# The heads phase of an mLSTM layer: memory products two slots sooner, chunk statistics behind each slot's urgent work, a third row buffer, and the last chunk's tiles in spent value room

## The chip, the cores and the metric

One core of a Trainium2 chip runs the whole program in one launch. The metric is device time in microseconds; before the change three runs gave a median of 3094.31 us (3094.05 to 3098.62). TensorE is PE in the profile (PEld its weight loads), VectorE DVE, ScalarE ACT, GpSimd POOL, and SyncE SP, which here only issues DMAs.

## The reference

Two layers on 1024 prompt tokens and 32 sample tokens (8 batches of 4). Each layer is a token mixer, a layer norm, a squared-ReLU MLP and a layer norm; layer 0 mixes by a Conformer convolution, layer 1 by mLSTM with 4 heads of width 512. The change lies in the mLSTM heads:

```python
num = a * (q @ C) + s @ v            # s = (q k^T) * exp(d - m), causal
den = a * (q @ n) + sum(s)
h = num / max(|den|, exp(-m))
C_new = decay * C + (k * w)^T @ v    # prompt and 8 sample states, [512, 512] each
# per head, over its 512 columns:
hn = (h - mean(h)) * rsqrt(var(h) + eps) * norm_g
out = sigmoid(o_pre) * (hn + skip * xc)      # then out @ w_down
```

## The kernel before

The four heads run one after the other. A head first makes queries, keys and values and the prompt's own memory (some 50 us), then goes through 16 **slots**, in which three kinds of work are laced together. The order on every engine is written out by hand in `phase_b_pe`, `phase_b_act`, `phase_b_dve` and `phase_b_pool`: each engine takes its list in order, and semaphores tie the lists.

- **Attention steps.** 14 steps (`SLOTS`; slots 2 and 3 have none and add the carried memory instead, `carried`, 8 matmuls twice a slot). For step r PE makes `scores` (L1567), DVE weights them (`weighted`, L2053, tile PT), ACT rounds them (`high`, L1819, PH), DVE takes the rest (`low`, L2075, PL) and PE adds `values` (L1582 to L1584, 12 matmuls). Scores run two steps ahead of values. ACT's `weights` (L1828, exponentials) run three ahead.
- **Memory products.** 16 halves of the 8 sample states (`HALVES`), by `memory` and `new_memory`: the first half of a batch starts with `old_memory` (L1614, PE reads the state tile CT), and each half has two products (L1639), which DVE folds into CT (`update`, L2045). States come and go by DMA through three CT buffers, 1 MB each way.
- **Chunk statistics.** The prompt's rows come in four chunks of 256 tokens (tc 0, 1, 2 and END), the sample rows are DEC. When a chunk's last step is done (`LAST`: slots 1, 5, 9, 15), a chain runs over the engines: `denominators` (PE L1603), `den_part` (ACT L1705), `bound` (DVE L2177); `raw_out` (ACT L1723 or L1720) takes the numerators out of PSUM; `sum_tiles` 1 (DVE), `head_mean` (PE L1448), `center` (DVE L2206), `square` (ACT L1731), `sum_tiles` 2 (DVE, ends in L2199), `head_var` (PE L1453), `root` (ACT L1737, a table load and a square root into SD), `inverse` (DVE L2211), `normalise` (DVE L2217), `gain` (ACT L1746), `skip` (DVE L2232), `gate` (DVE L2240), and `out_store` by POOL (L1403). The denominator of one chunk shares its PSUM bank with the variance of the chunk before, so `denominators` waits for that chunk's `root` (semaphore hsd). The statistics of DEC and END are finished inside the next head, between its query and token products (L1479, L1502).

Before, the chunks alternate between two row buffers HT0 and HT1, and `raw_out` waits until the row stored two chunks earlier has left (o_out). After the last head comes the down projection (`down`, `product` at L447 to L449; `beside` puts the last statistics among its matmuls). POOL splits its weight panels (`split_panel`, L432 and L434) into space that the heads used, so each panel also waits for whatever lay there.

## Time and profile before

| | us |
|---|---|
| median of three runs | 3094.31 |
| the profiled execution | 3095.94 |
| its span in the profile | 3094.2 |
| PE busy | 2968.4 (96%) |
| DVE busy | 1687.0 (55%) |
| ACT busy | 846.0 (27%) |
| POOL busy | 1069.2 (35%) |

The profile is one execution. A busy share is a mean over stages: the heads phase runs from about 1590 to 2142 us of the span, the down projection and the second MLP follow. A row of the timeline gives start and duration in us, engine, line, what is written and read, and in square brackets how long the engine had been idle and what ended it.

### The profile page before, as it was taken

Reading aid. Unit: us, or ns where it says so; the run is one execution under the profiler, and the core shown is the slowest. Engines: PE = TensorE matmul, PEld = TensorE weight load, DVE = VectorE, ACT = ScalarE, POOL = GpSimd, SP = SyncE. Lnnn points to the kernel's source line nnn. Section 1 sums busy time; section 2 is a strip of 40 time slices with the busy share of each in tenths; the row PEclk is TensorE's granted clock in tenths of the full one; section 3 lists DMA queues with packets and bytes.
Section 4 is the critical chain, followed back from the end, with each engine's and each line's share of the span. In section 5 each row is a group of like instructions: output and inputs, shape, how many; then the busy total and the mean of one; then the engine's idle time right before and its main releaser. Section 6 shows DMA issues by size and latency. Waiting matters only on the chain.

```text
span 3094.2 us, 50087 instructions
## 1 busy us (share of the span) xinstructions
PE 2968.4 (96%) x19348; PEld 2748.6 (89%) x19348; DVE 1687.0 (55%) x2551; ACT 846.0 (27%) x1491; POOL 1069.2 (35%) x742
## 2 busy tenths in 40 slices
PE   7998899999999999999989989897999999999997
PEld 7885789999999998999967768675998999999997
DVE  5877445544444455344357887877226444444445
ACT  4000542222212224111144434434006122222211
POOL 3232023555565523333200111102332365555553
PEclk9999899999999999999989999998999999999999
DMA  8555211111111113433244563839310111111121
GB/s 229 138 142 141 80 50 42 40 42 50 51 54 47 55 35 108 141 105 104 90 171 178 188 229 137 298 119 328 118 42 28 55 55 41 37 44 48 53 75 57
DMA packets 276673, 313.20 MB, mean 101 GB/s; under 512 B 25733, under 2 KB 217477, under 8 KB 275314
## 3 DMA queue, kind: packets, MB, share of 16 engines
q1 hardware_dynamic: 257777, 250.82, 26.7%
q10 hardware_dynamic: 13048, 40.28, 3.4%
q0 software_dynamic: 5712, 20.19, 1.8%
q8 instruction: 97, 1.59, 0.2%
q14 instruction: 39, 0.32, 0.0%
HBM read 219.91 MB, written 92.19 MB: 101 GB/s over the span
## 4 chain that ended last, share of the span: by engine, by line
PE 82%; DVE 8%; ACT 3%; issue 3%; DMA 2%; PEld 1%; POOL 0%; SPq 0%; another core or an unknown queue 0%; ACTq 0%; DVEq 0%; POOLq 0%; PEldq 0%
PE ps L447 19%; PE ps L448 19%; PE ps L449 19%; PE ps L882 3%; PE ps L881 3%; PE ps L883 3%; PE ps L1502 2%; PE ps L1567 2%; PE ps L2564 2%; PE ps L1523 1%; PE ps L1593 1%; PE ps L1525 1%; PE ps L1524 1%; DVE CT L2045 1%; PE ps L1639 1%
## 5 line engine op out<-in xcount | busy, mean ns | idle before, releaser
L447 PE MATMUL ps<-AH,WH 128*128 128x352 f32 x3072 | 999.1, 325 | 4.9 <-POOL WL L434 2.0
L449 PE MATMUL ps<-AH,WL 128*128 128x352 f32 x3072 | 985.3, 321 | 0.0
L448 PE MATMUL ps<-AL,WH 128*128 128x352 f32 x3072 | 985.2, 321 | 0.0
L447 PEld LDWEIGHTS ps<-AH,WH 128*128 128x128 f32 x3072 | 576.7, 188 | 30.3 <-issue 23.9
L448 PEld LDWEIGHTS ps<-AL,WH 128*128 128x128 f32 x3072 | 577.9, 188 | 1.1 <-issue 0.2
L449 PEld LDWEIGHTS ps<-AH,WL 128*128 128x128 f32 x3072 | 576.9, 188 | 0.0
L432 POOL TENSOR_SCALAR WH<-RAW 128x1024 fp32r<-128x1024 f32 x152 | 181.0, 1191 | 950.5 <-PEq L454 751.4
L434 POOL TENSOR_TENSOR WL<-RAW,WH 128x1024 fp32r<-128x1024 f32 x152 | 401.1, 2639 | 12.7
L1105 DVE TENSOR_TENSOR X<-X,ps 128x352 f32<-128x352 f32 x432 | 225.1, 521 | 264.6 <-PE ps L883 134.1
L996 ACT ACTIVATE SGF<-ps 128x352 f32<-128x352 f32 x192 | 88.9, 463 | 679.7 <-PE ps L449 679.6
L1057 DVE TENSOR_TENSOR HR<-SGF 128x352 f32<-128x352 f32 x144 | 92.7, 644 | 288.5 <-ACT SGF L996 286.6
L447 PE MATMUL ps<-HH,WH 128*128 128x352 f32 x768 | 249.6, 325 | 0.0
L449 PE MATMUL ps<-HH,WL 128*128 128x352 f32 x768 | 246.3, 321 | 0.0
L448 PE MATMUL ps<-HL,WH 128*128 128x352 f32 x768 | 246.0, 320 | 0.0
L742 POOL TENSOR_TENSOR WL<-RAW,WH 128x1024 fp32r<-128x1024 f32 x48 | 117.2, 2441 | 182.1 <-ACT WH L768 181.1
L2994 DVE SCALAR_TENSOR_TENSOR CB<-U,PR,CB 128x32 f32<-128x32 f32 (+3 forms) x180 | 155.4, 922 | 0.7
L447 PEld LDWEIGHTS ps<-HH,WH 128*128 128x128 f32 x768 | 144.1, 188 | 2.7 <-issue 2.3
L448 PEld LDWEIGHTS ps<-HL,WH 128*128 128x128 f32 x768 | 144.3, 188 | 0.4
L449 PEld LDWEIGHTS ps<-HH,WL 128*128 128x128 f32 x768 | 144.0, 187 | 0.0
L758 POOL TENSOR_TENSOR WL<-RAW,WH 128x1024 fp32r<-128x1024 f32 x48 | 116.9, 2435 | 45.0 <-ACT WH L771 44.0
L881 PE MATMUL ps<-HH,WH 128*128 128x352 f32 x384 | 123.6, 322 | 0.0
L882 PE MATMUL ps<-HL,WH 128*128 128x352 f32 x384 | 123.6, 322 | 0.0
(376 smaller groups left out, 4921.6 us busy)
## 6 DMA issues: line engine op xcount, KB each, us to landing
RAW<-in_ffn_w SPq DMA_DIRECT2D x128, 512.0 KB, 3.8
CT<-in_state_mlstm_C SPq DMA_DIRECT2D x32, 1024.0 KB, 6.8
out_C_s<-CT SPq DMA_DIRECT2D x32, 1024.0 KB, 7.7
RAW<-in_ml_w_in SPq DMA_DIRECT2D x32, 512.0 KB, 3.9
RAW<-in_conv_w_pw SPq DMA_DIRECT2D x24, 512.0 KB, 8.3
STK<-u_scratch SPq DMA_DIRECT2D x64, 184.0 KB, 3.8
xc_scratch<-XC ACTq DMA_DIRECT2D x16, 528.0 KB, 2.7
so_scratch<-SO ACTq DMA_DIRECT2D x16, 528.0 KB, 3.7
```

The lines of the kernel that those rows point to most:

```text
L432: pool.tensor_scalar(WH[:, k % 4], RAW[:, k % 2], 1.0, 0.0, ALU.mult, ALU.add).then_inc(w_hi, 1)
L434: pool.tensor_tensor(WL[:, k % 4], RAW[:, k % 2], WH[:, k % 4].bitcast(F32), ALU.subtract).then_inc(w_split, 1)
L447: pe.matmul(ps[:, bank, 0:CW], wh[:, k, cols], hi[:, k, cs], start=(k == 0), stop=False)
L448: pe.matmul(ps[:, bank, 0:CW], wh[:, k, cols], lo[:, k, cs], start=False, stop=False)
L449: mm = pe.matmul(ps[:, bank, 0:CW], wl[:, k, cols], hi[:, k, cs], start=False, stop=(k == nk - 1))
L742: pool.tensor_tensor(WL[:, 2 * g % 4], raw, WH[:, 2 * g % 4].bitcast(F32), ALU.subtract).then_inc(w_split, 1)
L758: pool.tensor_tensor(WL[:, (2 * g + 1) % 4], raw, WH[:, (2 * g + 1) % 4].bitcast(F32), ALU.subtract).then_inc(w_split, 1)
L881: pe.matmul(ps[:, bank, 0:CW], wh, hi(k), start=(start and k == 0), stop=False, skip_group_check=True)
L882: pe.matmul(ps[:, bank, 0:CW], wh, lo(k), start=False, stop=False, skip_group_check=True)
L883: mm = pe.matmul(ps[:, bank, 0:CW], wl, hi(k), start=False, stop=(k == 1), skip_group_check=True)
L1105: dve.tensor_tensor(x, x, ps[:, bank, 0:CW], ALU.add).then_inc(F.acc, 1)
L2994: ins = dve.scalar_tensor_tensor(y, x(t), w, y, ALU.mult, ALU.add)
```

## The change

The memory halves move two slots ahead and are spread: one half each in slots 0 and 1, two each in slots 2 and 3, one each in 4 to 13. Each chunk's denominators move one slot later, to the head of the slot, and the chain behind them one slot later too (on DVE behind the slot's updates and weighted scores, where before most of it stood ahead of them). The next head's block weights move from slot 12 to slot 0. The rows of chunk 2 lie in the first half of XO0 in place of HT0, so the gates' load for END waits for the store of chunk 2. In the last head, END's rows (HTL) and its loads (XOL) lie where the values were, and `raw_out` of END waits for no store; POOL splits the first two panels before it stores chunk 2 and splits the next two before it stores DEC and END. `head_mean` of DEC goes from ahead of the down projection to the middle of its first product.

```diff
-        HALVES = {2: (0, 1), 3: (2, 3), 4: (4, 5)} | {q: (q + 1,) for q in range(5, 15)}
-        IS_STEP = 13
+        HALVES = {0: (0,), 1: (1,), 2: (2, 3), 3: (4, 5)} | {q: (q + 2,) for q in range(4, 14)}
+        IS_STEP = 12
@@ ht, xo_load
+            if tc == END and h == HEADS - 1:
+                return HTL[:]
+            return (HT0, HT1, XO0[:, 0], None, HT0)[tc][:, :, 0:TC[tc][1]]
+            if tc == END and h < HEADS - 1:
+                pool.wait_ge(o_out[0], 16 * (3 * h + 2))
+            elif tc == END:
+                pool.wait_ge(pv_mm, NS * HEADS)
@@ phase_b_pe
                 for n, tc in enumerate((0, 1, 2, END)):
-                    if q == LAST[tc] and n != 1:
+                    if q == LAST[tc] + (tc != END):
                         denominators(n, FINAL[tc])
...
-                if q == LAST[1]:
-                    denominators(1, FINAL[1])
...
-                    if q == LAST[tc] + 3:
+                    if q == LAST[tc] + 4:
                         head_var(pe, h, tc)
@@ raw_out
-            if row_half(h, tc) and tc != DEC:
-                wait(act, o_out[1], 16 * (2 * h + (tc == END)))
-            else:
-                wait(act, o_out[0], 16 * (3 * h + (0, 0, 1, 0, 2)[tc]))
+            if tc < 2:
+                wait(act, o_out[1], 16 * 2 * h)
+            elif tc == 2:
+                wait(act, hskip, 5 * h)
+            elif tc == DEC:
+                wait(act, o_out[0], 16 * 3 * h)
+            elif h < HEADS - 1:
+                act.wait_ge(o_out[0], 16 * (3 * h + 1))
@@ phase_b_act
-                    if n == 2:
+                    if n == 3:
                         square(act, h, tc)
-                    if n == 3:
+                    if n == 4:
                         root(act, h, tc)
-                    if q == LAST[tc] + 4:
+                    if q == LAST[tc] + 5:
                         gain(act, h, tc)
@@ phase_b_dve: taken from the slot's head
-                    if n == 2:
-                        center(dve, h, tc)
-                    if n == 3:
-                        sum_tiles(dve, h, tc, 2)
-                    if n == 4:
-                        inverse(dve, h, tc)
-                    if n == 6:
-                        gate(dve, h, tc)
@@ behind the first update and weighted
-                    if q == LAST[tc] + 1:
+                    if n == 1:
                         sum_tiles(dve, h, tc, 1)
+                    if n == 5:
+                        inverse(dve, h, tc)
@@ at the slot's end
+                    if n == 2:
+                        center(dve, h, tc)
+                    if n == 3:
+                        sum_tiles(dve, h, tc, 2)
-                    if n == 4:
+                    if n == 5:
                         normalise(dve, h, tc)
-                    if n == 5:
+                    if n == 6 and not (tc == 2 and h == HEADS - 1):
                         skip(dve, h, tc)
+                    if n == 7:
+                        gate(dve, h, tc)
-                if q == 12:
+                if q == 0 and h < HEADS - 1:
@@ behind the last slot
+            if h == HEADS - 1:
+                skip(dve, h, 2)
+            gate(dve, h, 2)
```

Three places show how it moves instructions; head 1 is the one shown. First, PE around the denominators of chunk 1. The names are PS for the summed weights, SQH for the squares' sums, XCH and QT for keys and queries, CT for a state. Before:

```order
5248 L1614 MATMUL ps<-CT,QZ 32x512 [waits ct_in0]
5249 L1614 MATMUL ps<-CT,QZ 32x512 x3
5250 L1639 MATMUL ps<-VM,WKS 128x512 [waits upd_ev,vm_done]
5251 L1567 MATMUL ps<-QT,XCH_133 128x256 [waits p_done]
5252 L1567 MATMUL ps<-QT,XCH_133 128x256 x3
5253 L1603 MATMUL ps<-PS,ones_63 128x256 [waits hsd,hcent,psum_done]
5254 L1639 MATMUL ps<-VM,WKS 128x512 [waits upd_ev]
```

And in the change (the first 12 matmuls behind the variance are step 3's values):

```order
5255 L1648 MATMUL ps<-VM,WKS 128x512 [waits upd_ev]
5256 L1462 MATMUL ps<-SQH,ones_h 128x256 [waits hsum]
5257 L1591 MATMUL ps<-PH,VH 128x128 [waits p_lo]
...
5269 L1612 MATMUL ps<-PS,ones_63 128x256 [waits hsd,hcent,psum_done]
5270 L1623 MATMUL ps<-CT,QZ 32x512 [waits ct_in1]
5271 L1623 MATMUL ps<-CT,QZ 32x512 x3
5272 L1648 MATMUL ps<-VM,WKS 128x512 [waits upd_ev,vm_done]
5273 L1576 MATMUL ps<-QT,XCH_133 128x256 [waits p_done]
```

The denominators stood behind a state's products and a step's scores; now they stand ahead of both, 12 narrow matmuls behind the variance whose root they wait for.

Second, DVE at the end of the head, from the last weighted scores to the sums of DEC (SQD, DND) and END (SQH). Before:

```order
973 L2075 TENSOR_TENSOR PL<-PT,PH 128x128 [waits pv_mm,p_hi]
974 L2217 TENSOR_TENSOR HT_157<-HT_157,RST 128x1024 [waits hrst]
975 L2045 SCALAR_TENSOR_TENSOR CT<-CT,ROWB,ps 128x512 [waits upd_mm] x2
976 L2232 SCALAR_TENSOR_TENSOR HT_157<-XCH_133,PRM,HT_157 128x256 [waits hgain]
977 L2232 SCALAR_TENSOR_TENSOR HT_157<-XCH_133,PRM,HT_157 128x256 x3
978 L2240 TENSOR_TENSOR HT_157<-HT_157,XO_154 128x1024 [waits xo_in0,hskip]
979 L2177 TENSOR_TENSOR DND<-DND,ROWB 128x32 [waits den_abs]
980 L2192 TENSOR_TENSOR SQD<-HTD 128x64 [waits num_ev,hvar]
```

In the change:

```order
977 L2086 TENSOR_TENSOR PL<-PT,PH 128x128 [waits pv_mm,p_hi]
978 L2223 RECIPROCAL RST<-SD 128x256 [waits hsd]
979 L2229 TENSOR_TENSOR XO_157<-XO_157,RST 128x1024 [waits hrst]
980 L2244 SCALAR_TENSOR_TENSOR XO_157<-XCH_133,PRM,XO_157 128x256 [waits hgain]
981 L2244 SCALAR_TENSOR_TENSOR XO_157<-XCH_133,PRM,XO_157 128x256 x3
982 L2189 TENSOR_TENSOR DND<-DND,ROWB 128x32 [waits den_abs]
983 L2204 TENSOR_TENSOR SQD<-HTD 128x64 [waits num_ev,hvar]
...
986 L2252 TENSOR_TENSOR XO_157<-XO_157 128x1024 [waits xo_in0,hskip]
```

The reciprocal stood ahead of the last step's scores; now it stands behind them, no update separates the chain's links any more, and DEC's sums follow the skip.

Third, POOL behind the last head. HT_157 in row 269 is chunk 2. Before:

```order
269 L1403 DMA out_scratch<-HT_157 128x4x256 [waits hout]
270 L1395 DMA XO_154<-xc_scratch 128x4x256 [waits hout]
271 L1396 DMA XO_154<-so_scratch 128x4x256
272 L432 TENSOR_SCALAR WH<-RAW 128x1024 [waits w_free,w_raw0,upd_mm,p_lo]
...
277 L1403 DMA out_scratch<-HT_157 128x4x256 [waits hout]
278 L432 TENSOR_SCALAR WH<-RAW 128x1024 [waits w_free,w_raw0,hvar,o_out0]
```

In the change, where XO_157 in row 273 is chunk 2:

```order
269 L434 TENSOR_SCALAR WH<-RAW 128x1024 [waits w_free,w_raw0,upd_mm,p_lo]
...
271 L434 TENSOR_SCALAR WH<-RAW 128x1024 [waits w_free,w_raw1,o_out1,dexp]
...
273 L1415 DMA out_scratch<-XO_157 128x4x256 [waits hout]
274 L1407 DMA XOL<-xc_scratch 128x4x256 [waits pv_mm,hout]
275 L1408 DMA XOL<-so_scratch 128x4x256
276 L434 TENSOR_SCALAR WH<-RAW 128x1024 [waits w_raw0,w_free,o_out0]
```

Two panels are split before chunk 2 is stored, and the third panel no longer stands behind the store of END.

## Rows read from the trace of the kernel before

**Rows 1.** The page: span and PE's share.
```profile
span 3094.2 us, 50087 instructions
PE 2968.4 (96%) x19348; PEld 2748.6 (89%) x19348; DVE 1687.0 (55%) x2551; ACT 846.0 (27%) x1491; POOL 1069.2 (35%) x742
```
**Rows 2.** Windows: stretch, its length, busy us (instructions) by engine, clock, DMA, GB/s.
```profile
1780.80:1862.20 81.40, 73.13 (x428) 55.38 (x428) 67.54 (x122) 32.13 (x68) 8.04 (x11) 0.98 0.71 246
1866.00:1916.00 50.00, 49.32 (x287) 41.19 (x285) 38.83 (x80) 24.02 (x52) 4.81 (x7) 1.00 0.42 145
2141.70:2154.90 13.20, 0.82 (x4) 0.60 (x4) 8.88 (x8) 1.08 (x4) 10.51 (x7) 0.60 1.03 411
```
**Rows 3.** PE's waits in head 1's slots, 1780 to 1863: total, times, longest.
```profile
PE ps L1453 <- DVE SQH L2199: 3.1, 2, 1.6
...
PE ps L1603 <- ACT SD L1737: 1.8, 1, 1.8
```
**Rows 4.** Timeline of the weight loads of PE, head 1, slots 4 to 10.
```profile
1800.05 0.16 PEld L1614 LDWEIGHTS ps<-CT,QZ 128*32 128x32 f32 x8 [0.35 <-issue]
...
1825.08 0.30 PEld L1453 LDWEIGHTS ps<-SQH,ones_h 128*128 128x128 f32 x2 [2.05 <-DVE SQH L2199]
1828.96 0.30 PEld L1603 LDWEIGHTS ps<-PS,ones 128*128 128x128 f32 x2 [1.96 <-issue]
...
1830.87 3.17 PEld L1567 LDWEIGHTS ps<-QT,XCH 128*128 128x128 f32 x8
...
1835.85 1.73 PEld L1567 LDWEIGHTS ps<-QT,XCH 128*128 128x128 f32 x8
```
**Rows 5.** Timeline of DVE, head 1, slot 8.
```profile
1824.60 0.43 DVE L2199 SCALAR_TENSOR_TENSOR SQH<-DN,SQH 128x256 f32<-128x256 f32 x1
1824.94 0.74 DVE L2045 SCALAR_TENSOR_TENSOR CT<-CT,ROWB,ps 128x512 f32<-128x512 f32 x1
1825.60 0.42 DVE L2053 TENSOR_TENSOR PT<-ps,DT 128x256 f32<-128x256 f32 x1
```
**Rows 6.** Timeline of ACT, head 1, slot 8.
```profile
1826.05 0.41 ACT L1819 CAST PH<-PT 128x256 fp32r<-128x256 f32 x1 [3.04 <-DVE PT L2053]
1826.36 0.69 ACT L1828 ACTIVATE DT<-ROWB,BT 128x128 f32<-128x128 f32 x2
1827.08 1.28 ACT L1737 ACT_TABLE_LOAD   x1
1828.37 0.47 ACT L1737 ACTIVATE SD<-ps,tiny 128x256 f32<-128x256 f32 x1
```
**Rows 7.** Groups by line in head 1's slots: busy us, mean ns, idle before.
```profile
L2211 DVE RECIPROCAL RST<-SD 128x256 f32<-128x256 f32 x3 | 5.2, 1749 | 1.7 <-ACT SD L1737 1.7
...
L1746 ACT ACTIVATE HT<-HT,PRM 128x256 f32<-128x256 f32 x12 | 5.1, 499 | 1.4 <-DVE HT L2217 1.4
L2232 DVE SCALAR_TENSOR_TENSOR HT<-XCH,PRM,HT 128x256 f32<-128x256 f32 x12 | 5.0, 477 | 0.5 <-ACT HT L1746 0.5
```
**Rows 8.** Timeline of PE's weight loads where head 2 begins.
```profile
1863.94 0.32 PEld L1448 LDWEIGHTS ps<-SQD,ones_h 128*128 128x128 f32 x2 [0.28 <-issue]
...
1868.57 0.30 PEld L1453 LDWEIGHTS ps<-SQD,ones_h 128*128 128x128 f32 x2 [0.70 <-DVE SQD L2199]
```
**Rows 9.** PE's waits from 2140 to 2300 us.
```profile
PE ps L447 <- ACT HT L1720: 7.5, 1, 7.5
PE ps L1448 <- DVE SQD L2194: 4.9, 1, 4.9
```
**Rows 10.** Timeline from 2143 us: the last END rows, the third panel's first product.
```profile
2154.17 1.08 ACT L1720 COPY HT<-ps 128x512 f32<-128x512 f32 x2 [12.12 <-DMA out_scratch<-HT]
...
2184.21 0.40 PE L447 MATMUL ps<-AL,WH 128*128 128x352 f32 x1 [3.61 <-POOL WL L434]
```
**Rows 11.** The chain that ended last, head 3: start, us, what.
```profile
2084.10 8.96 DMA out_C_s<-CT
2093.08 15.23 DMA CT<-in_state_mlstm_C
```

More of the change, by code:

```diff
@@ L1284, in halves_at @@
             return [(n // 2, n % 2) for n in HALVES.get(q, ())]
-        def row_half(h, tc):
-            return 1 if tc == 1 or tc == END and h < HEADS - 1 else 0
         def store_sem(h, tc):
@@ L1369, in ht @@
         def ht(h, tc):
-            return HTD[:] if tc == DEC else HT[row_half(h, tc)][:, :, 0:TC[tc][1]]
+            if tc == DEC:
+                return HTD[:]
+            if tc == END and h == HEADS - 1:
+                return HTL[:]
+            return (HT0, HT1, XO0[:, 0], None, HT0)[tc][:, :, 0:TC[tc][1]]
         def squares(tc):
@@ L1377, in summed, with xo @@
             return 10 * h + (2 * tc + n if tc < 3 else 5 + 2 * n + (tc == END))
-        def xo(tc, m):
-            return (XOD0, XOD1)[m][:] if tc == DEC else XO[tc % 2][:, m if tc != 1 else 0, :, 0:TC[tc][1]]
+        def xo(h, tc, m):
+            if tc == DEC:
+                return (XOD0, XOD1)[m][:]
+            if h == HEADS - 1 and tc == END:
+                return XOL[:, m]
+            if h == HEADS - 1 and tc == 2 and m == 0:
+                return XCL[:]
+            return XO1[:, 0] if tc == 1 else XO0[:, m]
         def reloaded(h, tc):
@@ L1422, in phase_b_pool @@
             vm(2)
-            vm(3)
-            vm(4)
-            vm(5)
+            for b in range(3, 7):
+                vm(b)
             out_store(pool, h, 0)
             xo_load(pool, h, 2)
-            vm(6)
             vm(7)
             out_store(pool, h, 1)
-            xo_load(pool, h, 3)
-            out_store(pool, h, 2)
-            xo_load(pool, h, 4)
+            xo_load(pool, h, DEC)
             if h < HEADS - 1:
+                out_store(pool, h, 2)
+                xo_load(pool, h, END)
                 out_store(pool, h, DEC)
@@ L1442, in head_mean @@
             pe.wait_ge(num_ev, 5 * h + tc + 1)
-            if tc in (DEC, END):
-                pe.wait_ge(den_abs, 5 * h + tc + 1)
+            pe.wait_ge(den_abs, 5 * h + tc + 1)
             if tc != DEC:
@@ L2492, in _ @@
             split_panel(pool, NP_D + 1, NR_D // 2 + 1, 1, NQ_D + 1)
+            out_store(pool, HEADS - 1, 2)
+            xo_load(pool, HEADS - 1, END)
+            pool.wait_ge(o_out[0], 16 * 11)
+            split_panel(pool, NP_D + 2, (NR_D + 2) // 2 + 1, 2, NQ_D + 2)
+            pool.wait_ge(hvar, 20)
+            split_panel(pool, NP_D + 3, (NR_D + 3) // 2 + 1, 3, NQ_D + 3)
             out_store(pool, HEADS - 1, DEC)
             out_store(pool, HEADS - 1, END)
-            pool.wait_ge(o_out[0], 16 * 12)
-            pool.wait_ge(hvar, 20)
-            for k in range(2, 4):
-                split_panel(pool, NP_D + k, (NR_D + k) // 2 + 1, k, NQ_D + k)
             with pool.Fori(1, 4) as i:
@@ L2691, in beside @@
                 if (c, h, k) == (0, 0, KT // 2):
+                    head_mean(pe, HEADS - 1, DEC)
                     pe.wait_ge(wd_lo, 2)
@@ L2713, in down @@
                         between(c, n - 6)
-            head_mean(pe, HEADS - 1, DEC)
             pe.wait_ge(upd_ev, 4 * DEC_B * HEADS)
```

22 lines of the change are left out of this document (11 added, 11 removed).

## Prediction

> **What bounds the kernel now.** I read the page first: PE is busy for 96% of a span of 3094.2 us [rows 1], so almost everywhere the time is PE's own work, and a change of order can only give or take the places where PE waits. Then the windows over one head. In head 1's slots PE is busy 73.1 of 81.4 us and DVE 67.5; right behind them, where the next head makes its queries and tokens, PE is busy 49.3 of 50 us [rows 2]. So the slots hold some 8 us of PE idle per head, and whatever delays PE at a head's edge is paid in full, as there is no idle behind it to absorb it. Then the waits. In the slots PE waits 3.1 us in two variances for DVE's sums and 1.8 us in one set of denominators for ACT's square root [rows 3]; the timeline puts these at 1825.08 and 1828.96 [rows 4]. The last place is behind head 3: from 2141.7 to 2154.9 PE is busy 0.8 of 13.2 us, at a mean clock of 0.60 [rows 2]. There it waits 4.9 us for the sums of DEC, then 7.5 us for ACT's copy of END's numerators, and later 3.6 us for the third weight panel [rows 9, 10]. The copy itself had waited 12.1 us for a DMA, the store of chunk 2's rows out of the buffer it writes [rows 10].
>
> **The tail of the heads phase.** With its own buffer the END copy no longer waits for a store. What is late next: ACT's order is gain of chunk 2, DEC's numerators and denominators, the second rounding of the down projection's input, END's denominators, END's copy. In the new order (worked out below) chunk 2's gain ends 0.9 us behind PE's last value product, the other four take about 2.9 us, and PE starts the down projection 3.5 to 4 us behind its last value product: at about 2145.8 in before's clock, counted without the three heads ahead, against 2154.9. `head_mean` of END in that product will wait 2 us, since DVE now does skip and gate of chunk 2 ahead of END's sums. The third panel waits for chunk 2's store and no longer for END's; issued near 2149.5 it should have landed and been split by 2165, before the six first products end at about 2171.6, so the 3.6 us go too. Before, the seventh product starts at 2184.2 [rows 10]. That is -12.6 us; a clock drop of 3.4 us just behind it, worth 1.7, may go with the wait. I take **-14 us** for the tail, last head's own slots included; its bounds are 0 (the copy is held by something else, such as the rounding) and -16.0, the sum of the three waits [rows 9, 10].
>
> **The slots.** I walked head 1 through the new lists by hand, each instruction starting when its engine is free and its inputs are there, with durations and latencies from the trace: an update 0.66 (from 1824.94 to 1825.60), weighted scores 0.4 behind their matmuls, a step's scores 1.73, and so on [rows 4 to 7]. The starting point is the end of the first two scores, 1780.8, which the change leaves alone.
>
> *Gains.* Slots 0 and 1 take one memory half each, whose four updates (2.6 us) fall where DVE waited for PE. Slot 4 starts at 1802.4 in place of 1800.0 [rows 4], with two more halves done, which are about 1.9 us of PE and 2.6 us of DVE. So the start is worth up to 0.2 us where PE holds and nothing more; the rest of the gain must come from shorter waits later.
>
> *Losses.* (1) The denominators. In the old order those of chunk 1 stand behind a state's products and a step's scores and do not wait at all; only chunk 2's do, 1.8 us [rows 3]. From DVE's start on the weighted scores (1825.60) to the end of the root (1828.37 + 0.47) are 3.24 us: rounding, two exponentials, table load, root [rows 5, 6]. PE then starts 0.12 us later [rows 4]. In the new order root and variance sit in the slot before the denominators, for chunk 1 and chunk 2 alike, and that slot ends with a narrow step: behind its scores PE has only one memory product, the variance and 12 narrow matmuls, together 1.9 us, against 0.4 + 3.24 + 0.12 = 3.8 us on the other side. PE thus waits at least 1.9 us, and 2.3 to 2.5 where DVE starts that weighting behind the sums. And the wait is not hidden: DVE has done its short slot and can't go on, since its next update needs the memory product behind the denominators (some 2 us further), so DVE idles 3.8 us in slots 5 and 9 each. Before it idled 1.7 us for SD once [rows 7]. (2) DVE's `inverse` now stands ahead of the next chunk's first sum, which holds PE's mean by 1.5 us twice. (3) DVE's sums 2 at a slot's end wait for `square`, which stands behind rounding and exponentials on ACT, so the variance still waits 0.6 to 1.9 us each. (4) The head's end. Before, the variance of chunk 2 stood a slot earlier; now it is in slot 13 and behind it follow root, reciprocal 1.75, normalise 1.2, gain 1.7 and skip 1.7 with nothing between, then DEC's sums [rows 7]: 9.9 us, while PE has 7.8 us until `head_mean` of DEC. It waits 2.1 us there, 1.4 more for END's (gate and the query weights are ahead of it), and 0.5 more for DEC's variance.
>
> *The walk's times*, new against old: slot 4 at 1802.4 against 1800.0; the end of the denominators' wait in slot 6 at 1813.8; slot 10 at 1837.3 against 1835.7, where 1.5 us of the old figure was the lower clock (eight scores in 3.17 against 1.73 [rows 4]); `head_mean` of DEC 1867.7 against 1863.9; the variance of DEC 1873.5 against 1868.6 [rows 8]. That is +4.9 us for head 1 and, as heads 0 and 2 had no such clock drop, +6.4 each: **+17.7 us** for three heads. Each figure may be off by 3 us, as small errors add up along the list. The last head's +5 is inside the tail.
>
> *The table load.* The ACT rows show the load taking 1.28 us, begun 0.03 us behind the exponentials and followed by the root at once [rows 6]. The Trainium skill (ScalarE: Activation LUTs, What ACT_TABLE_LOAD costs) has such a load and a drain beside it, 2.66 us for a switch. By that, the wait of the denominators would be 1.4 us longer at each of 8 places, 11 us in all; the trace shows no drain here, so this isn't in the sum.
>
> *The clock.* Where PE waits often it was granted the lower level: 0.60 in the stretch of the tail [rows 2], and behind the two waits of slots 8 and 9 in head 1. More waits in the slots make more such drops likely; the one drop seen in head 1 cost 1.5 us, so I add **+2 us** (bounds 0 and 8 x 1.5 = 12).
>
> *At nothing.* The block weights in slot 0 (1.9 us on DVE) are covered, as DVE waits there for PE; uncovered they cost 1.9 per head. The states' DMAs: from one store's issue to the landing of the load behind it 24.2 us went by in head 3 [rows 11], and the new order needs the fifth state 21 us after that store, but the stores and loads of chunk 0's rows, 1.5 MB that ran in that stretch, now come later. 0, at worst 3 us. The gates' load for END now waits for chunk 2's store but is wanted only some 30 us into the next head; 0. Moving waits between semaphores of stores that are long done: 0.
>
> **Sum.** 17.7 - 14 + 2 = +5.7, of which I take 5: the profiled execution, 3095.94 us, becomes 3101. It stands 1.6 above the median, which becomes **3099 us**.
>
> **Rivals.**
> - *The slots get faster* (faster than before). The mechanism would be that DVE, not the chain of roots, is what holds PE in slots 4 to 12: then four halves' updates moved into DVE's idle start give back about 2.6 us, and the variances' 3.1 us per head go [rows 3]. For it: DVE is busy 67.5 of 81.4 us [rows 2], nearly as much as PE. Against: the denominators' waits, which the row at 1828.96 shows and the lists double. It would give -5 per head for three heads, -14 in the tail: 3065; half of it, with the slots even, 3080. Decisive is whether the denominators of chunks 1 and 2 wait over 2 us.
> - *The slots lose more* (slower). The idle spells of both engines bring the low clock in every head, and the last head's END mean and rounding hold the down projection: +8 per head, -8 in the tail, 3110. The clock's row for the slots (0.98 now) would be under 0.96.
> - *The tail gains nothing.* The down projection's start would be held by DVE's and ACT's longer queue as long as by the store: then 17.7 + 2 remain, 3114. Against it: the store alone accounts for 12 us of ACT's wait [rows 10].
>
> **How the numbers follow.** The forecast's case (slots +4 to +7 per head, tail -11 to -16) 0.55; its own range is 3089 to 3108. Faster or even slots 0.30; slots lose more 0.10; tail gains nothing 0.05. A measurement of this kernel can tell about 0.2%, or 6.2 us, from no change. Of the forecast's case, spread about +5, half lies within 6.2 and most of the rest above: slower 0.38 in all, no change 0.32, faster 0.30. The range leaves out the deep end of the faster rival and the slowest cases: 3080 to 3111.
>
> **What would show it.** In the new profile: PE's waits for SD at the denominators, 4 to 6 us per head with two of over 2 us (1.8 in one now); the wait for SQH's variance nearly as long as before; a new wait for DEC's and END's sums of 3 to 4 us where each next head starts; DVE idle for PE's memory product near 3.8 us twice a head; heads that start 5 to 7 us further apart; the wait for END's copy down from 7.5 to about 4 and none for the third panel. The forecast is wrong if the heads come closer together than now, which would show that the chain through ACT is hidden, or if the END copy still ends a long wait for a DMA.

## The result, and the profile after

The changed kernel takes 3117.30 us (median of four runs, 3116.66 to 3120.58) against 3096.07 for the kernel before: a ratio of 1.0070, 95% interval 1.0053 to 1.0088. It is slower by 21 us; 3099 with a range of 3080 to 3111 was forecast. The profiled execution took 3116.66 us.

The page's first lines, answering to [rows 1]: PE has 12 us more busy time with the same 19348 matmuls, and the span is 20.7 us longer, so about 9 us of it is idle.

```profile
span 3114.9 us, 50098 instructions
PE 2980.4 (96%) x19348; PEld 2759.4 (89%) x19348; DVE 1688.4 (54%) x2551; ACT 844.2 (27%) x1491; POOL 1071.4 (34%) x742
```

The cleanest measure of a head is from its first scores to those of the next head, since nothing ahead of them was moved. The windows (stretch, length, busy us of each engine, clock, DMA share, GB/s) for heads 0 to 2, first before, then after:

```profile
1640.33:1778.20 137.87, 128.88 (x760) 101.75 (x759) 111.59 (x214) 60.06 (x126) 15.09 (x21) 1.00 0.59 205
1778.20:1917.74 139.54, 130.59 (x759) 102.84 (x759) 111.60 (x214) 60.06 (x126) 15.09 (x21) 0.99 0.59 203
1917.74:2055.66 137.92, 128.93 (x760) 101.76 (x759) 111.62 (x214) 60.07 (x126) 15.11 (x21) 1.00 0.59 205
```
```profile
1638.56:1785.54 146.98, 133.25 (x760) 104.46 (x759) 110.37 (x214) 59.48 (x126) 15.70 (x21) 0.97 0.55 193
1785.54:1932.43 146.89, 133.39 (x760) 104.37 (x759) 110.38 (x214) 59.51 (x126) 15.71 (x21) 0.97 0.54 193
1932.43:2079.27 146.84, 133.45 (x760) 104.39 (x759) 110.37 (x214) 59.52 (x126) 15.71 (x21) 0.97 0.55 193
```

A head takes 8.5 us longer (440.71 against 415.33 us for three): 4.6 us more idle of PE and 3.9 us more busy time for the same matmuls, at a clock of 0.97 in place of 1.00 or 0.99. From head 3's first scores to the end it is 1035.6 us against 1038.5, only 2.9 less. Up to head 0's first scores the profiled execution is 1.8 us shorter; nothing ahead of that place was changed, and over the profiles of this document it lies anywhere from 1637.5 to 1642.1 us, so this is spread and no gain.

The longest of PE's waits in head 1 after, with total, times and longest single wait (before: [rows 3], with one wait of 1.8 us for SD):

```profile
PE ps L1462 <- DVE SQH L2211: 3.8, 3, 2.1
PE ps L1457 <- DVE SQH L2206: 3.5, 3, 1.6
PE ps L1612 <- ACT SD L1748: 2.3, 2, 1.9
PE ps L1457 <- DVE SQD L2206: 1.4, 1, 1.4
```

And the places of the timeline that answer to [rows 4 to 6] and [rows 8], head 1: the weight loads of PE at the denominators of chunk 1, at the variance of chunk 1 and the denominators of chunk 2, and at the DEC mean, then DVE, then ACT.

```profile
1814.31 1.72 PEld L1576 LDWEIGHTS ps<-QT,XCH 128*128 128x128 f32 x8
...
1820.84 0.30 PEld L1612 LDWEIGHTS ps<-PS,ones 128*128 128x128 f32 x2 [2.03 <-issue]
...
1823.18 2.73 PEld L1576 LDWEIGHTS ps<-QT,XCH 128*128 128x128 f32 x8
...
1842.13 0.36 PEld L1462 LDWEIGHTS ps<-SQH,ones_h 128*128 128x128 f32 x2 [2.50 <-DVE SQH L2211]
...
1846.01 0.50 PEld L1612 LDWEIGHTS ps<-PS,ones 128*128 128x128 f32 x2 [0.53 <-issue]
...
1877.48 0.30 PEld L1457 LDWEIGHTS ps<-SQD,ones_h 128*128 128x128 f32 x2 [1.90 <-ACT HT L1734]
```
```profile
1817.48 0.41 DVE L2064 TENSOR_TENSOR PT<-ps,DT 128x256 f32<-128x256 f32 x1
...
1823.85 0.75 DVE L2056 SCALAR_TENSOR_TENSOR CT<-CT,ROWB,ps 128x512 f32<-128x512 f32 x1 [4.63 <-PE ps L1648]
...
1849.61 0.75 DVE L2056 SCALAR_TENSOR_TENSOR CT<-CT,ROWB,ps 128x512 f32<-128x512 f32 x1 [5.21 <-PE ps L1648]
```
```profile
1818.95 1.28 ACT L1748 ACT_TABLE_LOAD   x1
1820.25 0.47 ACT L1748 ACTIVATE SD<-ps,tiny 128x256 f32<-128x256 f32 x1
```

The chain is the one that the prediction walked: weighted scores at 1817.48, root done at 1820.72, denominators at 1820.84, 3.36 us in all (3.24 + 0.12 predicted). PE stands still for 2.0 us, and DVE, which cannot go on before the memory product behind the denominators, for 4.6 and 5.2 us in the two slots. Then the clock: 2.3 us behind the denominators the eight loads of a step's scores take 2.73 us, where they took 1.72 ahead of the wait. The windows over head 1's slots and over its two low stretches show which level it is: 3.4 us at 0.52 and 6.8 us at 0.51, about half, which is the lower one (1.2 GHz). Ahead of the first of them PE had stood still for 2.0 us, at the denominators. The second begins right behind another wait, that of chunk 1's variance for DVE's sums (2.1 us of PE, ended at 1842.13). It lies over the values ahead of the denominators of chunk 2, which then wait for SD only 0.4 us. Both stretches stand at the same places in all three heads.

```profile
1785.54:1867.50 81.96, 71.42 (x392) 52.96 (x391) 61.33 (x116) 27.73 (x58) 7.64 (x10) 0.94 0.63 226
...
1822.00:1825.40 3.40, 3.40 (x14) 1.95 (x7) 0.75 (x1) 0.00 (x0) 0.00 (x0) 0.52 1.03 408
1842.50:1849.30 6.80, 6.43 (x25) 3.78 (x24) 1.90 (x5) 4.05 (x7) 0.28 (x1) 0.51 0.94 339
```

The tail, answering to [rows 9, 10]: PE at the start of the down projection, at END's mean and at the second pair of panels, then DVE in the stretch between the last slots and END's mean.

```profile
2173.22 0.63 PE L449 MATMUL ps<-AL,WH 128*128 128x352 f32 x1 [5.46 <-ACT HTL L1731]
...
2181.23 0.77 PE L1457 MATMUL ps<-SQH,ones_h 128*128 128x256 f32 x1 [3.02 <-DVE SQH L2206]
...
2206.13 0.43 PE L449 MATMUL ps<-AL,WH 128*128 128x352 f32 x1 [0.76 <-DVE X L3198]
```
```profile
2165.68 3.40 DVE L2229 TENSOR_TENSOR XO<-XO,RST 128x1024 f32<-128x1024 f32 x1
...
2177.07 1.53 DVE L2204 TENSOR_TENSOR SQH<-HTL 128x512 f32<-128x512 f32 x1
2178.64 2.44 DVE L2206 TENSOR_TENSOR SQH<-SQH 128x256 f32<-128x256 f32 x1
```

END's copy has no DMA in front of it and the third panel makes nobody wait, but other waits stand where these were, and three of DVE's operations take two to six times what they take elsewhere (1.2, 0.68 and 0.42 us). From the first product to the first one of the second panel pair, before and after (the row at 2184.21 [rows 10] and the one at 2206.13), PE is idle about as long, with the wait for END's mean where the one for the panel was; but it is busy 3.4 us longer, for three matmuls more and at a lower clock (0.84 in place of 0.95):

```profile
2154.90:2184.21 29.31, 25.70 (x150) 25.34 (x151) 20.55 (x32) 9.80 (x15) 5.09 (x5) 0.95 0.42 149
```
```profile
2173.22:2206.13 32.91, 29.13 (x153) 28.36 (x153) 31.31 (x36) 9.80 (x15) 16.05 (x11) 0.84 0.67 257
```

### The profile page after: what moved, and what is told of

Its sections match the earlier page's. It is cut to its first block, busy times and chain, and to the rows that moved or that the text cites. A ratio compares the mean times of both kernels' runs of the same rounds, so it can differ in the third digit from the quotient of the medians.

```text
span 3114.9 us, 50098 instructions
## 1 busy us (share of the span) xinstructions
PE 2980.4 (96%) x19348; PEld 2759.4 (89%) x19348; DVE 1688.4 (54%) x2551; ACT 844.2 (27%) x1491; POOL 1071.4 (34%) x742
## 4 chain that ended last, share of the span: by engine, by line
PE 82%; DVE 9%; ACT 4%; issue 3%; PEld 1%; DMA 1%; POOL 0%; SPq 0%; another core or an unknown queue 0%; ACTq 0%; DVEq 0%; PEldq 0%; POOLq 0%
PE ps L449 19%; PE ps L450 19%; PE ps L451 19%; PE ps L884 3%; PE ps L883 3%; PE ps L885 3%; PE ps L1576 2%; PE ps L1511 2%; PE ps L2578 2%; PE ps L1623 1%; PE ps L1532 1%; DVE RST L2223 1%; PE ps L1602 1%; PE ps L1534 1%; PE ps L1533 1%
## 5 line engine op out<-in xcount | busy, mean ns | idle before, releaser
L450 PE MATMUL ps<-HL,WH 128*128 128x352 f32 x768 | 246.0, 320 | 0.0
L2056 DVE SCALAR_TENSOR_TENSOR CT<-CT,ROWB,ps 128x512 f32<-128x512 f32 x128 | 93.8, 740 | 55.8 <-PE ps L1648 55.8
```

The lines of the kernel that those rows point to most:

```text
L450: pe.matmul(ps[:, bank, 0:CW], wh[:, k, cols], lo[:, k, cs], start=False, stop=False)
L2056: dve.scalar_tensor_tensor(x, x, ROWB[:, a0:a0 + 1], ps[:, UPD[k % 2], :], ALU.mult, ALU.add).then_inc(upd_ev, 1)
```

## The experiments

Eleven kernels, each timed in five rounds beside the kernel before. The table gathers them. "Head" is the mean of the three spacings from first scores to first scores, "busy" PE's share of it and "idle" the rest; "product" is the first matmul of the down projection and "end" the end of the span, both from head 3's first scores, in us of the profiled execution. That one execution can lie off the median: it took 3107.59 us for e5, 3119.51 for e7 and 3084.37 for e9.

| kernel | median | ratio, 95% interval | head | busy | idle | product | end |
|---|---|---|---|---|---|---|---|
| before | 3096.07 | 1 | 138.4 | 129.5 | 9.0 | 99.2 | 1038.5 |
| changed | 3117.30 | 1.0070 (1.0053 to 1.0088) | 146.9 | 133.4 | 13.5 | 94.0 | 1035.6 |
| e1: denominators back | 3090.08 | 0.9978 (0.9969 to 0.9987) | 139.8 | 129.9 | 9.9 | 88.3 | 1030.0 |
| e2: halves alone | 3095.51 | 0.9999 (0.9990 to 1.0008) | 139.5 | 129.5 | 10.0 | 94.6 | 1035.8 |
| e3: changed, old halves | 3100.75 | 1.0013 (1.0004 to 1.0022) | 143.1 | 131.2 | 11.9 | 90.6 | 1032.1 |
| e4: tail alone | 3083.45 | 0.9959 (0.9945 to 0.9972) | 138.5 | 129.5 | 9.0 | 88.1 | 1026.8 |
| e5: filler | 3112.54 | 1.0051 (1.0038 to 1.0064) | 145.2 | 133.8 | 11.4 | 91.2 | 1032.6 |
| e6: split late | 3117.44 | 1.0066 (1.0053 to 1.0078) | 146.5 | 131.5 | 15.1 | 94.7 | 1036.5 |
| e7: root first | 3113.89 | 1.0053 (1.0039 to 1.0068) | 146.4 | 132.5 | 13.9 | 94.8 | 1036.5 |
| e8: e4 and chunk 2's denominators | 3076.05 | 0.9932 (0.9920 to 0.9944) | 136.0 | 128.6 | 7.4 | 85.1 | 1026.5 |
| e9: e8 and the halves | 3080.72 | 0.9954 (0.9940 to 0.9967) | 138.8 | 129.8 | 8.9 | 90.4 | 1026.2 |
| e10: e8, variance behind | 3076.58 | 0.9942 (0.9929 to 0.9956) | 136.6 | 129.3 | 7.3 | 85.2 | 1024.8 |
| e11: e8, down first | 3075.64 | 0.9937 (0.9923 to 0.9951) | 135.9 | 128.5 | 7.4 | 82.3 | 1024.9 |

**The denominators (e1).** In the changed kernel, the denominators of chunks 0 to 2 go behind the slot's state products and scores:

```diff
-                for n, tc in enumerate((0, 1, 2, END)):
-                    if q == LAST[tc] + (tc != END):
-                        denominators(n, FINAL[tc])
+                if q == LAST[END]:
+                    denominators(3, FINAL[END])
...
                     scores(r + 2)
+                for tc in range(3):
+                    if q == LAST[tc] + 1:
+                        denominators(tc, FINAL[tc])
```

> The changed kernel with one edit: the denominators of chunks 0 to 2 stand behind the next step's scores in their slot, as those of chunk 1 did before. Theory (the chain weighted scores, rounding, exponentials, table load, root into the denominators holds both PE and DVE in slots 6 and 10 and brings the two low-clock spells per head): the two waits of about 2 us go and DVE's idle in slots 5 and 9 falls from 5 us to under 2; heads 5 to 6 us closer together (141 to 142 us apart in place of 146.9), time 3092 to 3098. Rival 1 (the longer chain at the head's end, from the variance of chunk 2 to DEC's sums, is what costs): heads at most 2 us closer, 3109 or more. Rival 2 (the earlier memory halves cost, by DMA or DVE load): no change, 3115 to 3118.

3090.08 us (3084.55 to 3098.14), 27 us less than the changed kernel: the place of one kind of matmul, 12 in the whole program, decides the sign. The theory holds, and the gain is more than it said (3092 to 3098 us, heads 141 to 142 apart; here 139.8). In head 1 DVE's two idle spells of 4.6 and 5.2 us are 1.2 us each. PE has no wait for SD left, its idle is 9.9 us a head in place of 13.5, and its busy time falls back from 133.4 to 129.9 us.

**The halves alone (e2).** The kernel before with the two lines of `HALVES` and `IS_STEP` of the change.

> The kernel before with only the memory halves two slots sooner (and the copy of the sample sums one slot sooner); statistics, buffers and tail as before. Theory (the statistics' placement costs, the halves don't): heads 1 to 3 us closer together than before's 138.4 on average, time 3084 to 3093. Rival 2 (the halves cost): slower than before, 3100 or more.

3095.51 us: no difference, which neither side expected. The trace shows why it is none: a head gets 1.1 us longer, since PE, with less left to do in the last slots, now waits for DEC's sums where the next head begins, and behind head 3's first scores 2.7 us are won back. Before, this wait was there once, 4.9 us behind the last head [rows 9]; in e2 it is:

```profile
PE ps L1448 <- DVE SQD L2194: 14.9, 4, 7.2
```

**The statistics alone (e3).** The changed kernel with the old `HALVES` and `IS_STEP`.

> The changed kernel with the memory halves in their old slots. Theory (statistics' placement costs, halves give a little): heads as far apart as in the changed kernel or up to 3 us further, 3117 to 3128. Rival 2 (the halves cost): heads back near 138 to 140, 3092 to 3097.

3100.75 us, between the two ranges and in neither. Against the tail alone (e4, 3083.45) the later statistics cost 17 us, and moving the halves as well costs another 16.6, though by themselves they cost nothing. Both parts draw on the same cover: a head grows by 4.6 and then by 3.8 us. PE's wait for the prompt's variances is 15.0 us in the changed kernel and 5.1 here; its wait for SD is 10.8 and 13.6.

**The tail alone (e4).** The kernel before with the new buffers, POOL's new order and `head_mean` of DEC in the product, and with the slots as before.

> The kernel before with only the new buffers, the new order on POOL and the mean of DEC inside the down projection; halves and statistics in their old slots. Theory (the tail is worth what the missing wait for a store gives, but DVE and ACT are then late and DVE runs slower beside POOL's splits): the down projection starts 5 to 8 us sooner after head 3's first scores (99.2 before), heads unchanged at 138.4 apart, time 3086 to 3091. Rival (the tail edit is worth the 2.9 us that the changed kernel shows behind head 3, whatever the slots): 3092 to 3094.

3083.45 us (3082.05 to 3086.14), 12.6 less than before: the heads are the same to 0.1 us, and nearly all of the gain lies behind head 3's first scores, 11.7 us. That is more than the theory's range: the down projection starts 11.1 us sooner, where 5 to 8 were expected. The END copy waits for no DMA any more.

**Filling the wait (e5).** The changed kernel with a redundant set of scores in PE's wait for SD, four matmuls (eight in the trace) at two places of each head:

```diff
                     if q == LAST[tc] + (tc != END):
+                        if tc in (1, 2):
+                            scores(r + 2, True)
                         denominators(n, FINAL[tc])
```

> The changed kernel with one more set of scores for the step that comes next, computed ahead of the denominators of chunks 1 and 2 (slots 6 and 10) and computed again at its own place: the first result is overwritten. It is 1.73 us of matmuls at two places of each head, where PE waits up to 1.9 us for SD; nothing else moves. In the changed kernel a head takes 8.5 us longer than before, 3.9 us of it in PE's busy time (133.4 in place of 129.5 us for the same matmuls), the rest idle. Theory (the lower clock is brought by the idle of PE at the denominators): with that idle filled PE's busy time falls back by about 3.9 us less what the filler adds (3.5), the idle falls by 3 us, so the time falls by 1.5 to 4 us a head and the whole comes to 3102 to 3112 though PE does 13.8 us more work. Rival (the lower clock has another source, or the filler pushes the chain behind it): the filler is paid where it is longer than the wait, 0.5 us at each place and the variance behind it, and the clock row stays at 0.97: 3116 to 3128.

3112.54 us (3107.59 to 3114.73), beside 3116.64 to 3118.71 for e6, whose slots are the changed kernel's and which ran on the same chip: PE does 13.8 us more work and the kernel is 5 us faster. That is half a microsecond outside the theory's range, and on its side. The mean granted clock of its six executions is 0.986 to 0.990, that of the changed kernel's four 0.983 to 0.985. The rows below are of an execution of 3107.59 us. In it the stretch behind the denominators of chunk 1 is gone from every head, while the one behind the variance, whose wait the filler doesn't touch, is there in the second and third head (3.4 and 6.8 us) and not in the first:

```profile
1637.51:1781.31 143.80, 132.27 (x776) 104.69 (x775) 110.43 (x214) 59.43 (x126) 15.71 (x21) 1.00 0.57 197
1781.31:1926.44 145.13, 133.77 (x776) 105.92 (x775) 110.43 (x214) 59.47 (x126) 15.70 (x21) 0.99 0.55 195
1926.44:2073.20 146.76, 135.41 (x776) 107.52 (x775) 110.43 (x214) 59.48 (x126) 15.70 (x21) 0.98 0.56 193
```

At the full clock a head takes 143.8 us, 5.9 more than before at the full clock (137.87); the prediction's walk gave 6.4 for such a head. What lies between 143.8 and 146.9 is not the clock's for certain: the filler also shifts the waits behind it.

**POOL's split later (e6).** One line ahead of POOL's first panel in the tail of the changed kernel: `pool.wait_ge(hnorm, 5 * (HEADS - 1) + 3)`.

> The changed kernel, but POOL's first split of a down panel waits until DVE has normalised chunk 2 of the last head; nothing else moves. In the changed kernel that normalise took 3.40 us beside POOL's split (2164.50 to 2168.0) and 1.2 us elsewhere, and the gain, the four operations of ACT behind it and the first product of the down projection hang on it. Theory (the two engines hold each other up, and the tail's missing gain is partly that): the normalise takes 1.2 us again, the first product starts 2 us earlier behind head 3's first scores (92 in place of 93.95 us), total 3114 to 3116. Rival (POOL's panel is then late: it is split 2.3 us later, ends by 2170.4, and the second one and the stores behind it slip as well, or DVE's next operation is stretched in its place): no gain, 3117 to 3119.

3117.44 us: the rival. The normalise does take 1.23 us again (3.40 in the changed kernel), but a little later a sum of 32 columns takes 2.27 us, where it takes 0.19 elsewhere. DVE first, then POOL:

```profile
2166.43 1.23 DVE L2229 TENSOR_TENSOR XO<-XO,RST 128x1024 f32<-128x1024 f32 x1
2167.58 1.62 DVE L1896 TENSOR_TENSOR AH<-WR,AL 128x1408 fp32r<-128x1408 f32 x1
...
2170.31 2.27 DVE L2206 TENSOR_TENSOR SQD<-SQD 128x32 f32<-128x32 f32 x1
```
```profile
2167.91 2.19 POOL L434 TENSOR_SCALAR WH<-RAW 128x1024 fp32r<-128x1024 f32 x1 [5.19 <-issue]
2170.18 2.35 POOL L436 TENSOR_TENSOR WL<-RAW,WH 128x1024 fp32r<-128x1024 f32 x1
```

DVE's sum begins 0.13 us behind POOL's subtraction and ends 0.05 us behind its end (2172.58 and 2172.53). But END's copy does not hang on that sum. The gain of chunk 2 now ends 0.9 us behind PE's last value product in place of 3.1; then ACT's rounding, two operations ahead of the copy, waits for a load of stored rows (WR), which made nobody wait in the changed kernel:

```profile
2171.11 1.36 ACT L1888 CAST AL<-WR 128x1408 fp32r<-128x1408 f32 x1 [1.47 <-DMA WR<-out_scratch]
```

So PE's wait for END's copy fell by 0.6 us, no more. END's two sums took 1.52 and 2.44 us as in the changed kernel, and the time stayed.

This run also shows how clock and waits trade, as its slots are the changed kernel's. PE's waits for SD, first in the changed kernel, then here:

```profile
PE ps L1612 <- ACT SD L1748: 10.8, 8, 1.9
```
```profile
PE ps L1612 <- ACT SD L1748: 14.4, 8, 1.9
```

Here the stretch behind chunk 1's denominators is at the full clock in heads 0 to 2, and chunk 2's denominators wait 1.9 us in each of them, where the changed kernel waits 0.3 to 0.6. A head is 0.4 us shorter for it, no more.

**The root ahead of the exponentials (e7).** In ACT's list of the changed kernel `root` stands ahead of `weights`.

> The changed kernel with the root (and its table load) ahead of the exponentials of the step in ACT's list, in the slots where both stand. It takes 0.69 us (two exponentials) out of the chain from the weighted scores to SD at each of the denominators' waits and of DVE's waits behind them, and adds nothing. Theory (the chain through ACT sets the slots' time): PE's wait for SD falls from 10.8 us to about 5 in all, the head takes 1 to 2.5 us less, total 3107 to 3114. Rival (the waits are for DVE's sums and variances, and SD's is only where they show): the waits move to SQH, 3115 to 3119.

3113.89 us (3110.13 to 3119.51), 3.5 less than e6 beside it and at the theory's upper end, but two of its six executions took over 3119 us, more than any of e6's, so the gain is not certain. The longest wait for SD falls from 1.9 to 1.3 us, as the 0.69 us of two exponentials say. The total falls only from 10.8 in the changed kernel to 9.9, not to 5; against e6, where the low clock hides less of these waits, it falls by 4.5. A head is 0.5 us shorter in place of 1 to 2.5, in a profiled execution of 3119.51 us.

**Chunk 2's denominators behind the scores (e8).** The slots as before, the tail new, and one more chunk where chunk 1 stood:

```diff
-                    if q == LAST[tc] and n != 1:
+                    if q == LAST[tc] and n not in (1, 2):
                         denominators(n, FINAL[tc])
...
-                if q == LAST[1]:
-                    denominators(1, FINAL[1])
+                for tc in (1, 2):
+                    if q == LAST[tc]:
+                        denominators(tc, FINAL[tc])
```

> Slots of the kernel before with the new tail, as in the run that took the tail alone (3083.45), and chunk 2's denominators put behind a state's products and a step's scores, where chunk 1's stand already. Theory (what costs at the denominators is that they stand ahead of PE's and, through it, DVE's work): PE's four waits of 1.8 us for SD (7.1 in all) go, and the time falls by 4 to 7 us to 3077 to 3080. Rival (the head's time there is DVE's, which waits 1.7 us for SD in the same slot anyway): 3082 to 3085.

3076.05 us (3075.76 to 3077.11), 7.4 less than e4, just over the theory's 4 to 7, and 20 less than before. The row `PE ps L1612 <- ACT SD L1750: 7.1, 4, 1.8` of e4 has no answer here, and the heads fall from 137.9, 139.5 and 137.9 us to 135.9, 135.9 and 136.2. The middle one loses its low stretch with the wait:

```profile
1640.94:1776.88 135.94, 128.59 (x760) 101.92 (x759) 111.10 (x214) 60.05 (x126) 15.04 (x21) 1.00 0.60 208
1776.88:1912.77 135.89, 128.36 (x759) 101.84 (x759) 111.10 (x214) 60.05 (x126) 15.03 (x21) 1.00 0.60 208
1912.77:2048.94 136.17, 128.80 (x760) 101.89 (x759) 111.34 (x214) 60.05 (x126) 15.04 (x21) 1.00 0.59 208
```

**The halves with the denominators out of the way (e9).** e8 with the change's `HALVES` and `IS_STEP`.

> The kernel of the run before (slots as before the change, new tail, chunk 2's denominators behind the scores; 3076.05 us) with one part of the change more: the memory halves two slots sooner. It differs from the changed kernel with its denominators back (3090.08 us) only in where the statistics stand. Theory (moving the halves is worth nothing by itself: the head's last slots get thin, and the head then ends at the statistics' chain, as the halves alone showed with heads 1.1 us longer): 3075 to 3082, and the statistics' later places then make up most of the 14 us to 3090. Rival (with no denominators in the way the earlier halves pay at last): 3066 to 3073. Second rival (the halves are what is left of the loss): 3084 to 3090.

3080.72 us (3077.69 to 3087.43), 4.7 more than e8: the earlier halves pay nowhere. A head takes 2.8 us longer; PE waits 7.7 us in three places for DEC's sums, and 3.9 us for a state's load (2.4 in e8). e1, 3090.08, differs from it in the statistics' places and in the slot of the next head's block weights. These two are thus the other 9.4 us; no run takes them apart, and both kernels scatter (3077.69 to 3087.43 and 3084.55 to 3098.14).

**The variance behind the values (e10).** In e8, `head_var` goes behind `values(r)`, and `inverse` on DVE behind the first weighted scores.

> The same 3076.05 us kernel with each chunk's variance matmul behind the step's values instead of ahead of them, and DVE's reciprocal of the root behind the slot's first update and weighted scores instead of ahead. PE waits for DVE's sums at the variance 11.8 us, 8 times. Theory (that wait is lost time of PE, which values that are ready could fill): 3066 to 3073. Rival (the root comes 1.5 us later, and DVE or the denominators wait for it instead): 3074 to 3081.

3076.58 us, the rival: the waits of 11.8 us for the variance fall to 0.8, and those for DVE's updates and means rise, from 10.6 to 14.2 and from 2.3 to 8.9 us.

**The down projection's operands first (e11).** In e8, `down_high(act, 0, 1)` goes behind `raw_out` of END and `down_low(dve, 0, 0)` ahead of chunk 2's `skip`.

> The same 3076.05 us kernel with the tail in another order: ACT rounds the second half of the down projection's input behind END's copy instead of ahead of it, and DVE makes the first half's remainder (AH) ahead of chunk 2's skip instead of behind its gate. In the 3076.05 us kernel the first product starts at 2134.07, 4.3 us behind PE's last values, released by AH; ACT's rounding had waited 1.9 us for a DMA and END's copy stood behind it until 2132.9. Theory: the first product starts at about 2130.9 (AH ready), and what follows moves with it: 3072 to 3074. Rival (the first panel pair ends at DVE's chain of END and the sums into X, which wait for POOL's third panel's neighbourhood and not for the start): 3075 to 3077.

3075.64 us (3074.20 to 3077.55) against 3076.05: the same. The first product does start 2.8 us sooner behind head 3's scores (82.3 in place of 85.1), but the second pair of panels starts where it did, 116.2 us behind them in both kernels. The rows of e11:

```profile
2129.95 0.40 PE L449 MATMUL ps<-AL,WH 128*128 128x352 f32 x1 [1.48 <-DVE AH L1897]
...
2163.80 0.43 PE L449 MATMUL ps<-AL,WH 128*128 128x352 f32 x1 [1.01 <-DVE X L3199]
```

The second is released by DVE's sums into X, which stand in DVE's list behind END's whole statistics. So the start of the down projection is not what bounds this stretch; by the row, the end of END's chain on DVE is, though no run shortens that chain.

**The sum of the parts.** Along one path through these kernels, by medians: new tail -12.6 (before to e4), chunk 2's denominators behind the scores -7.4 (e8), halves two slots sooner +4.7 (e9), statistics later +9.4 (e1), denominators ahead of the slot's work +27.2 (the changed kernel); together +21.3. The steps of 4.7 and 9.4 are less certain than the others, as said at e9. Another path through them (e4, e3, changed) gives +17.3 for the statistics with their denominators and +16.6 for the halves: the parts do not add up independently.

## Why the prediction was wrong

The sign and the mechanism of the slots were right, the size was 21 us in place of 5. In the profiled executions three heads came to +25.4 us where 19.7 were forecast, and the rest of head 3 with all behind it to -2.9 where 14 were; the 1.8 us ahead of head 0 make up the rest. Two terms of the sum failed: the tail's, short by 11.1 us, and the clock's, by 5.7.

- **The walk of the slots, +17.7: right in what it gave for a head, as far as it can be told from the clock.** The end of the wait in slot 6 was given as 1813.8 on before's clock; head 1 starts 7.34 us later after, which makes 1821.14, and the row stands at 1820.84. From there on head 1 loses what the walk did not have: `head_mean` of DEC comes at 1877.48 in place of 1875.04 (1867.7 + 7.34), the variance of DEC at 1883.26 in place of 1880.8. Without the low clock the head is 5.9 us longer than before (e5's first head, filler and all), 6.4 as walked. DVE's idle came as listed and longer: 4.6 and 5.2 against 3.8. The denominators' waits did not: 4 to 6 us a head with two of over 2 were named as the sign, and it was 2.2 to 2.5 us in heads 0 to 2, 1.9 for chunk 1 and 0.3 to 0.6 for chunk 2, as there the low clock had already held PE back; in e6 both are 1.9. That the denominators are the cause, e1 shows by taking them away, and e8 by doing the opposite of the change.
- **The clock, +2: failed.** What the walk leaves over is 7.7 us in three heads in place of 2 (25.4 measured, less the walk's 17.7; a difference, measured by no run of its own), with low stretches of 3.4 and 6.8 us in every one, where before had one of 3.4 in three heads. The term was taken from the one drop in the old trace, as if the number of drops would stay nearly the same; yet the sum itself had just doubled the waits that stand ahead of such drops. Its upper bound, 12 us, was right and was not used for the range. Where the low stretch falls on time that is waited anyway it costs little: e6's heads have less of it (131.5 us busy in place of 133.4) and 1.6 us more idle, and are nearly as long (146.5 and 146.9). So part of the 7.7 us may be waits that the walk had too short, and the runs don't divide it further.
- **The tail, -14: failed, and the larger miss.** Head 3 and what follows gave 2.9 us. The buffer did what was said: no copy waits for a store, and with the old slots the tail is worth 12.6 us (e4). The forecast put the first product at 2145.8 and the second panel pair near 2171.6, which are 90.1 and 115.9 us behind head 3's first scores; they came at 94.0 and 126.9. Three things were wrong. First, the last head's slots: 2145.8 less 3.5 to 4 us puts the last value product where it was before (2141.9), which leaves no room for the walk's +5. It came 2.2 us later than before, counted from head 3's first scores, and 4.5 later than in e4. Second, the first product starts 5.5 us behind the last value product and not 3.5 to 4, partly as normalise was slowed and with it chunk 2's gain (3.1 us behind in place of 0.9). Third, and most, 7 us between the first product and the second pair. The wait for the third panel, 3.6 us, was taken as a gain in full, but something stood right behind it: DVE's chain of END. In the changed kernel the mean of END waits 3.02 us at 2181.23, the clock is 0.84 in that stretch in place of 0.95, and the first product of the second panel pair is released by DVE's sums into X, at 126.9 us behind head 3's scores against 128.55 before [rows 10] and 118.0 in e4. e11 shows it by itself: 2.8 us sooner at the start are nothing at the second pair.
- **DVE beside POOL: not in the sum.** The chain behind the last root was walked with each operation's usual duration. POOL splits panels in just that stretch, and normalise took 3.40 us for 1.2, the two sums of END 1.53 and 2.44 for 0.68 and 0.42, DEC's skip 5.89 for 0.73. e6 shows that moving one split doesn't mend it: normalise is free again, a later sum of DVE is held in its place, and END's sums are held by the second panel as before. The trace of the kernel before had such rows already, DVE's bound of END at 2.56 us for 0.42 beside POOL's subtraction, and the forecast did not use them:

```profile
2148.09 2.56 DVE L2177 TENSOR_TENSOR DN<-DN,ROWB 128x256 f32<-128x256 f32 x1
```
```profile
2146.67 3.70 POOL L434 TENSOR_TENSOR WL<-RAW,WH 128x1024 fp32r<-128x1024 f32 x1
```

- **The table load: as the trace had it.** 1.28 us with the root 0.01 to 0.02 us behind it, at every one in the heads of the changed kernel; the longer switch weighed beside the sum did not show, and the result is not to be explained by it.
- **The rivals.** The result is nearest in kind to "the slots lose more", which had 0.10: +8 a head against 8.5 measured, but with -8 in the tail for -2.9. Its sign, a clock of the slots under 0.96, is met: 0.94 in head 1's (1785.54 to 1867.50). "The slots get faster" falls with e2 and e9: earlier halves are worth nothing there, and both put the new wait at the head's end, for DEC's sums. "The tail gains nothing" gave 3114, the nearest number, but not by its way: e4's tail gains 12.6 us. The block weights in slot 0, taken at nothing, were tested by no run of their own.

## What to carry to other kernels

When a wait is added to PE, walk what comes behind it twice, once at each clock level: a chain that leaves PE idle at a fixed place can bring the low level back there in every round of the loop, as it did here in one kernel and not in each of the others with the same waits. The price per round is then the wait plus up to half of the slow stretch, less what that stretch hides of other waits, and not an average over the old trace. Put an instruction that waits for another engine's long chain behind all work of its own engine that is ready, above all behind the work that a third engine needs; that was worth 27 us in the changed kernel (e1) and 7.4 us with the old slots (e8). A stall removed from a stretch is worth only the distance to the next release in it: name that release, from the trace, before counting the stall.

## What the runs showed of the hardware

A DVE operation with both inputs in SBUF that begins while POOL's subtraction of two SBUF tiles runs does not get slower in proportion: it ends when POOL's has ended plus at most its own time. A sum of 32 columns took 2.27 us in e6, ending 0.05 us behind POOL's; normalise, 1.2 us alone, took 3.40 in the changed kernel, beside a subtraction from 2165.64 to 2168.01, and ended 1.07 us behind it. The Trainium skill (SBUF — State Buffer, Who interferes with whom) has this as an exclusive lock on a port pair that GpSimd shares with DVE, where the order of issue decides who blocks, and counts a DVE instruction with two SBUF inputs among those that contend with a GpSimd instruction that reads SBUF; these rows agree. POOL is held in turn: its conversion of a panel takes 1.05 us elsewhere and 2.19 in e6, where it begins at 2167.91, behind DVE's remainder of 2167.58, and ends 0.9 us behind that one's end (2170.10 and 2169.20).

The lower clock in a loop is a matter of place, and sensitive: in the changed kernel both stretches stood at the same two places of heads 0 to 2, each right behind a wait of PE of some 2 us, while e6 and e7, with the same PE order in the slots, had one of 6.8 us in each of the three heads (e6), or one in the first and two in the others (e7). These are single executions. What makes it fall behind one wait and not behind another was not settled. A filler that only keeps PE at work went with a higher granted clock over all its executions (0.986 to 0.990 against 0.983 to 0.985) and with 5 us less (e5).
